# Loading the up and down weights of one more item as whole 2 MB transfers in a two-layer encoder with 32 experts

## The reference

```
for l in range(DEPTH):                                   # DEPTH = 2
    x = x + mixer_sublayer(x, ..., w_in[l], ..., w_out[l])
    x = x + hier_moe(rms_norm(x, norm2_g[l]), ..., w_gate[l], w_up[l], w_down[l])
...
def expert_block(args):                                  # inside hier_moe
    e, idx = args
    xb = xt[idx]
    return (jax.nn.silu(xb @ w_gate[e]) * (xb @ w_up[e])) @ w_down[e]
```

## Time and profile before

| | |
|---|---|
| median of three executions | 1164.03 us |
| the profiled execution | 1165.27 us |
| its span, first to last instruction | 1163.5 us |
| TensorE busy | 991.7 us, 85% of the span |
| read from HBM | 434.88 MB, mean 375 GB/s |
| granted TensorE clock, mean over the span | 0.928 of 2.4 GHz |

### The profile page before, as it was taken

How to read it: one execution, slowest core, us unless ns; L and a number is a source line. 1 busy time by engine, 2 the same in 40 slices (tenths; PEclk the granted TensorE clock), 3 DMA queues, 4 the chain that set the end, 5 groups by cost and what they waited for, 6 DMA issues and landing times.

```text
span 1163.5 us, 13755 instructions
## 1 busy us (share of the span) xinstructions
PE 991.7 (85%) x5418; PEld 466.8 (40%) x5418; DVE 327.1 (28%) x742; ACT 171.3 (15%) x440; POOL 51.7 (4%) x104
## 2 busy tenths in 40 slices
PE   9999999998887945649999999999969889474697
PEld 5556644453333412114355556444523334131142
DVE  4546543222120210102145565432212212101021
ACT  1344311110010100000013343111100101000000
POOL 2121100000000000000021211000000000000000
PEclk9999999998998987878999999999988989687799
DMA  9952979999999999999998237999999999999997
GB/s 313 350 244 109 360 287 419 425 426 428 427 428 426 429 428 388 429 425 423 400 396 302 109 149 322 341 416 426 427 427 428 428 427 430 426 429 428 425 421 298
DMA packets 61026, 436.86 MB, mean 375 GB/s; under 512 B 10800, under 2 KB 15072, under 8 KB 29984
## 3 DMA queue, kind: packets, MB, share of 16 engines
q1 hardware_dynamic: 60960, 435.95, 91.4%
HBM read 434.88 MB, written 1.30 MB: 375 GB/s over the span
## 4 chain that ended last, share of the span: by engine, by line
PE 64%; DMA 29%; DVE 3%; issue 1%; SPq 1%; POOL 1%; ACT 0%; DVEq 0%; POOLq 0%
PE bank L1032 31%; DMA ring<-in_w_up 11%; DMA ring<-in_w_down 11%; PE bank L753 9%; PE bank L1058 5%; DMA ring<-in_w_gate 5%; PE bank L880 5%; PE bank L993 5%; PE bank L712 2%; DMA work<-in_w_down 2%; PE bank L826 1%; PE bank L816 1%; PE bank L848 1%; SPq L498 1%; PE bank L1050 1%
## 5 line engine op out<-in xcount | busy, mean ns | idle before, releaser
L1032 PE MATMUL bank<-ring,work 128*32 128x512 f32 (+2 forms) x2608 | 476.3, 664 | 139.9 <-DMA ring<-in_w_up 51.7
L1032 PEld LDWEIGHTS bank<-ring,work 128*32 128x32 f32 (+2 forms) x2608 | 143.6, 130 | 406.7 <-issue 404.1
L753 PE MATMUL bank<-ring,hT 128*128 128x512 f32 (+1 forms) x384 | 128.2, 488 | 0.8 <-DVE hT L1382 0.8
L993 PE MATMUL bank<-work,h 128*128 128x128 f32 x704 | 89.9, 283 | 5.7 <-DVE work L1759 5.1
L993 PEld LDWEIGHTS bank<-work,h 128*128 128x128 f32 x704 | 85.2, 198 | 21.1 <-issue 14.4
L753 PEld LDWEIGHTS bank<-ring,hT 128*128 128x128 f32 x384 | 71.4, 190 | 48.2 <-issue 42.8
L1032 PE MATMUL bank<-work 128*32 128x512 f32 (+2 forms) x192 | 83.1, 621 | 5.4 <-DMA ring<-in_w_down 5.4
L1032 PE MATMUL bank<-kept,work 128*32 128x512 f32 (+2 forms) x176 | 81.7, 617 | 5.3 <-DMA ring<-in_w_up 5.3
L1789 DVE COPY work<-bank 128x512 f32<-128x512 f32 x22 | 15.2, 692 | 248.4 <-PE bank L1032 246.0
L1058 PE MATMUL bank<-work 128*128 128x512 f32 x176 | 81.4, 603 | 2.4 <-ACT work L1337 1.6
L1779 DVE TENSOR_TENSOR work<-work,bank 128x512 f32<-128x512 f32 x22 | 15.1, 688 | 237.3 <-PE bank L1032 237.3
(11 more groups left out here) (205 smaller groups left out, 683.1 us busy)
## 6 DMA issues: line engine op xcount, KB each, us to landing
ring<-in_w_gate SPq DMA_DIRECT2D x42, 2048.0 KB, 26.0
ring<-in_w_up SPq DMA_DIRECT2D x36, 2048.0 KB, 29.3
ring<-in_w_down SPq DMA_DIRECT2D x36, 2048.0 KB, 24.2
ring<-in_w_up SPq DMA_DIRECT2D x36, 1024.0 KB, 14.4
ring<-in_w_down SPq DMA_DIRECT2D x30, 1024.0 KB, 9.8
ring<-in_w_gate SPq DMA_DIRECT2D x26, 1024.0 KB, 8.2
ring<-in_w_in SPq DMA_DIRECT2D x8, 1536.0 KB, 13.2
ring<-in_w_out SPq DMA_DIRECT2D x8, 1024.0 KB, 17.1
```

The source lines that it names most:

```text
L753: last = matmul(bank[6 + i % 2][:, 0:c1 - c0], hT[:, k, t * P:t * P + P], group_in(l, gi)[:, k, c0:c1], start=(k == 0), stop=(k == KD - 1))
L993: last = nc.tensor.matmul(bank[k // 4][:, k % 4 * P:k % 4 * P + P], h_kc[:, t, k, :], pick[:, t, :], start=(t == 0), stop=(t == TT - 1))
L1032: last = nc.tensor.matmul(bank[b][e * w:e * w + w, :], lhs[:, k, e * w:e * w + w], rows(pos, k_count // 2)[:, kk, n * 512:n * 512 + 512], ...
```

## The change

Item i = 2 joins those that are loaded whole, but only for its up and down matrices; its gate matrices stay in 1 MB pieces. Nothing else in the code differs.

```
-WHOLE_FROM = 3
+
+WHOLE_FROM = 2
...
 def whole(i, r):
-    return i >= WHOLE_FROM and (i < NI - 1 or r < 2)
+    return (i > WHOLE_FROM or i == WHOLE_FROM and r >= 2) and (i < NI - 1 or r < 2)
```

## The result

| | before | after |
|---|---|---|
| median | 1164.48 us (11 executions, 1162.36 to 1167.39) | 1169.62 us (11 executions, 1168.81 to 1172.65) |
| ratio, with its 95% interval | | 1.0039 [1.003, 1.0048] |
| profiled execution | 1165.27 us, span 1163.5 | 1170.02 us, span 1168.2 |
| read from HBM, mean over the span | 375 GB/s | 373 GB/s |

The medians differ by 5.1 us, the ratio is worth 4.5 us (3.5 to 5.6); 5.3 us were forecast. The same bytes are read, so the engines must have stood still for longer. The page has it where it gives the time that the packets took as a share of the span; for the queue of the weights it was 91.4% of 1163.5 us before, and after it is

A forecast was written before the change was run, and what follows sets the result against it. DMA engines taken as the bound, the queue full behind item 2, so idle gaps are lost. Layer 0 +1.6, layer 1 +4.2, other traffic -0.5: +5.3 us on 1164.03, 1169.3 us; range 1165.5 to 1172.5 us.

The forecast's parts named there:

- The queue behind item 2 passes a delay on: Behind item 2 the DMA queue never runs dry, so a delay put into it comes out at its end.
- two gaps less the rate: Layer 1, item 2: idle 2.3 us and 2.5 us, less 0.6 us saved by larger transfers, +4.2 us.
- its 1.6 us: Layer 0, item 2: 2.2 us idle less 0.6 us saved by larger transfers, +1.6 us.
- The rate: Item 2, full queue: eight 2 MB transfers take 39.2 us, sixteen 1 MB ones 39.7 us; 0.5 to 0.6 us saved per layer.
- fixed cost of about 2.0 us for each transfer: Skill page's figure, 32 us saved over both layers; the rows disagree for a full queue; rival of a faster kernel, chance 0.04.
- The start on an empty queue: A 2 MB transfer on idle engines: 2.6 us before data moves, 7.5 us in all.
- Doubled with the bytes: Rival: start grows to 5.2 us for 2 MB, +11.0 us, 1175.0 us; chance 0.16 together with a milder form.
- The gap in layer 0, and two in layer 1: Engines idle at item 2's first up matrix in layer 0 (2.2 us), first two in layer 1 (2.3, 2.5 us).
- the turn of the ring: Layer 1: second up matrix gets pieces 16 and 17, the later free with item 1's round 2; 2.5 us idle.
- The sum: Both layers: 1.6 + 4.2 - 0.5 = +5.3 us, median 1169.3 us, 0.46% slower.
- Other traffic in the gaps: Part of about 1.8 us of other engine work can fall into the gaps; 0.5 us taken off over both layers.
- TensorE's rounds: Item 2's down rounds: in time by 0.8 us in layer 0; round 4 in layer 1 waits about 1 us, costing nothing more.

The follow-up runs named there:

- a forecast delay of 6.6 us: Against the kernel before, only item 2's down matrices loaded whole, in layer 1 only: median 1170.72 us, ratio 1.0057.
- down only: Against the kernel before, only item 2's down matrices loaded whole, in both layers: median 1176.0 us, ratio 1.0085.
- the old turn: Against the kernel before, item 2's up and down matrices loaded whole in layer 1 only: median 1166.93 us, ratio 1.0013.
- a third turn: Changed kernel with ties among free places decided the other way for four output-projection pieces of layer 1: 1172.15 us, ratio 1.005 against the kernel before.

## Why the prediction was right

**The queue behind item 2 passes a delay on.** Right for layer 1: the share there is 1.01 at the same GB/s as before, the forecast 4.2 us (two gaps less the rate) appear as +4.4 us in the trace, and a forecast delay of 6.6 us gave +6.6 us. The prediction's sentence that a layer's experts end when the last of their weights lands does not hold for layer 0. There TensorE waits for weights last at the gate matrices of the last item, some 45 us before the end, and in the profiled execution of before not even there. So for layer 0 the step from the queue to the end was not secured, and how much of its 1.6 us arrives is not shown. One reading of the slices was also off, without effect on the sum: they show nine tenths from the seventh to the twenty-first and from the twenty-sixth to the thirty-ninth.

**The rate.** As forecast it is worth next to nothing. The kernel that keeps the waits and undoes the merges is 1.4 us above the changed one by the ratios (5.9 against 4.5; 1.2 forecast), within the error of both. No run shows the fixed cost of about 2.0 us for each transfer that the Trainium skill's page DMA: Bandwidth & Descriptors states (section Anatomy of one DMA) and that the prediction turned into 32 us: sixteen transfers fewer made the kernel slower. The page measured it on transfers that GpSimd issues; these are issued by SyncE.

**The start on an empty queue.** Taken as 2.6 us, 7.5 us with the transfer. Measured 7.5, 7.9, 8.0 and 8.6 us in four cases (the last at 203.07 us with down only), and 9.6 us for the matrix issued at 766.54 us in the changed kernel. Only the one of 8.0 us had the queue to itself (the next issue came 7.3 us behind it), which leaves 3.1 us beside 4.9 for the data; whether the 9.6 us are the start's or those of the two transfers issued 3.4 and 3.9 us behind it is not shown. Doubled with the bytes it would have been 10.1 us. Nor do 2.6 us pass "before data moves": after the issue at 759.28 us the engines are all but still until 760 us, and move 229 GB/s in the microsecond from there,

```profile
758.00:760.00 2.00, 2.00 (x12) 0.72 (x10) 0.00 (x0) 0.00 (x0) 0.00 (x0) 1.00 0.10 41
760.00:761.00 1.00, 1.00 (x6) 0.29 (x4) 0.00 (x0) 0.00 (x0) 0.00 (x0) 1.00 1.13 229
```

and the gate piece ahead, whose data had all but ended at 758 us, was reported landed at 760.0 us. A part of the 2.6 us thus lies behind the data and not ahead of it. Counted from landing to landing the gap is the same.

**The gap in layer 0, and two in layer 1.** All three are there, at the places forecast, and of the size: 2.1, 2.5 and 2.3 us where 2.2, 2.3 and 2.5 were forecast. That the second one of layer 1 comes from the turn of the ring and not from the merge is shown twice: with the old turn it is absent (+1.4 us instead of +4.4 in the trace for that layer), with a third turn it moves.

**The sum.** 5.3 us forecast, 4.5 us (3.5 to 5.6) measured. Where the change reaches layer 0 too, the same working comes out too large in all eight kernels that were to lose something: 5.3 against 4.5, 1.8 against 0.9, 4.0 against 2.3, 13 against 9.9, 6.3 against 5.9, 4.3 against 3.1, 6.5 against 5.7 and 8.2 against 5.8; three of these (4.0, 13 and 8.2) lie outside their intervals. In the two kernels that change layer 1 alone it fits, 1.8 against 1.5 and 6.6 against 6.6. This points at layer 0 as the place where something is taken away, and the changed kernel's trace, with 4.4 us in layer 1, says the same. It is a pattern in differences that are mostly within the noise, and not shown. Other traffic in the gaps, for which 0.5 us was taken off, could take something too; that was not measured either. So the sum came out well in part because 1.6 us for layer 0, which may be too much, are a small share of it.

**TensorE's rounds.** Round 4 of item 2 in layer 1 waits 2.2 us for its matrices, where about 1 was forecast and before it waited for none. No run separates what this costs, but layer 1's +4.4 us leave little room beside the 4.2 of the gaps and the rate. TensorE's three largest groups of waits for weights, 137.5 us in the earlier trace rows, are now

```profile
PE bank L1033 <- DMA ring<-in_w_down: 62.1, 10, 9.4
PE bank L1033 <- DMA ring<-in_w_up: 54.8, 6, 10.8
PE bank L1033 <- DMA ring<-in_w_gate: 29.7, 6, 8.6
```

146.6 us. The 9.1 us more are twice what reaches the end.

## What to carry to other kernels

Where a queue of loads is full only just, and its issues wait for space, merging two loads means waiting for the later of two spaces; set the start of a transfer on an empty queue (here 2.6 to 3.7 us for 2 MB in four cases) against the saving in a full one (here less than 0.1 us for each merge by the rates of the earlier trace rows). Go through the issues one by one: the earliest moment that each one's data could move, against the moment the queue runs out. And when a planner hands out places in a ring, a change in one layer moves the places in the next; its cost there has to be read from the plan, not carried over.

## What was not expected of the hardware

The same 96 matmuls on the way to layer 0's last item took 15.4 us in one execution and 13.0 us in another, though the order of work is the same; over the last 32 of them the granted clock was 0.69 in the one and 1.00, the full 2.4 GHz, in the other. Of the twelve profiled executions nine took 3.84 us for these 32, three took 5.2 to 5.4 us. In the trace this hid a delay of 2.3 us. Whether so small a delay is in fact absorbed the timed executions do not tell; of 6.5 us most arrived. One profiled execution of each kernel is not enough to read a difference of 1 or 2 us over a long stretch.
